# Second mixer of a two-block model: rotary queries first, rotation on GpSimd, six output rows, another order of scaling and additions

## The chip, the cores and the metric

The kernel runs on one core of a Trainium2 chip. The metric is device time in microseconds (us) of one execution. The engines are named as the profile names them: PE (TensorE matrix products, with PEld its weight loads), DVE (VectorE), ACT (ScalarE), POOL (GpSimd) and SP (SyncE, which here only issues the transfers of weights).

## The reference

Two blocks of a small model are computed for 256 tokens of width 1024, in float32. The part that the change touches is the second mixer of the second block: attention over compressed keys and values (six heads), attention over a memory (four heads), a product with an output matrix whose result is added to x, and the norm that the next feed-forward network starts with.

```python
cq, q_mem = split(rms_norm(x, mix_norm) @ b_w_in, [256])
q = (rms_norm(cq, b_q_norm) @ b_w_uq).reshape(b, s, 6, 128 + 64)
q_nope, q_rope = split(q, [128])
q_rope = apply_rope(q_rope, cos, sin)        # x1*c - x2*s, x1*s + x2*c
# six heads, in blocks of 128 queries, causal by chunks of 64
sc = (q_nope @ k_nope.T + q_rope @ k_rope.T) * 192 ** -0.5
o_b = softmax(where(mask, sc, -inf)) @ v
# four heads over 256 memory tokens
o_m = softmax(q_mem @ k_mem.T * 64 ** -0.5) @ v_mem
x = x + concat(o_b, o_m) @ w_out             # 1024 x 1024
x = x + 0.5 * swiglu(rms_norm(x, ffn2_norm), w_gu, w_down)
```

## The kernel before

**Products in three parts.** Features lie on the 128 partitions and the 256 tokens along a row. Each large product is exact float32 put together from three fast products: a value is split into a rounded high part and the rest (`_hi`, `_lo`), and `triple` (L1742) issues high times high, low times high and high times low into one bank. ACT writes the high part (`split_hi`, L471, one copy a unit of weights), DVE subtracts it to get the low part (`split_lo`, L927). Small products (scores, turned probabilities, head outputs, the rotation) are plain float32 matmuls.

**Weights.** They stream through four slabs of raw memory, two units a slab, and rings of four units `w_hi` and `w_lo`. Unit u may be written when PE has used unit u - 4 (`unit_used`). `slot(u)` splits unit u + 4 on ACT and u + 3 on DVE. SP issues a slab when DVE has split the slab four earlier (`lo_ready`).

**Banks.** Products of tiles go to four banks `main`, tile t to bank t mod 4; `bank_of(t)` waits until tile t - 4 has been read out (`evac`). Scores go to `side0` and `side3` in turn, turned probabilities to `side1`, a head's output to `side2`.

**Order.** Nothing is scheduled by a planner: each engine executes its own list, written out by hand, and the lists meet in semaphores. Around the change the lists stand in the last part of each engine's function: ACT L872 to L908, DVE L1527 to L1594, POOL L1719 to L1731, PE L2285 to L2384.

**A head.** PE issues `scores(a)`; DVE takes the row maxima (`row_maxima`, L970; for the six heads it adds the mask in the same pass, L987); ACT exponentiates (`exps`, L507) and sums; DVE multiplies by the inverse sum (`normalise`, L1000, two multiplications at L1007); PE turns the probabilities (`turn_probs`, L1803, shown as L1812); ACT copies them out (`copy_pt`, L520); PE forms the head's output (`outputs`, L1820, shown as L1838); ACT and DVE split it (`cat_hi` L868, `cat_lo` L1538). `MEM_B` to `MEM_B + 3` are the memory heads, `MLA` to `MLA + 5` the six others.

**The output matrix.** It is laid out in eight units. The first four hold a row block each (128 input features, all eight output tiles: `out_row`), for the inputs 6, 7 (memory) and 0, 1 (heads). The other four hold, for a pair of output tiles, the inputs 2 to 5 (`out_pair`). When a pair of tiles is complete DVE adds it to x (L1585), ACT scales the sum into the next network's high input (L499) and squares it (L495), DVE makes the low input (L959) and POOL adds up the squares (L1731). The network's first unit is eight `triple`s, one for each tile of x, each waiting for its low input; behind it PE sums the squares over the partitions (`norm_sum`, L1770), and goes on with the second unit.

## Time and profile before

| what | us |
|---|---|
| median of three runs | 1303.97 (1302.57 to 1303.99) |
| the profiled execution | 1301.14 |
| its span | 1299.4 |
| busy PE | 1245.8 (96% of the span) |
| busy DVE | 868.7 (67%) |
| busy ACT | 710.7 (55%) |
| busy POOL | 121.4 (9%) |

The profile shows one execution. "Span" is from the first instruction to the last; the 1.74 us beside it lie around the kernel. PE is busy nearly throughout, and the chain that ended last runs 85% through PE and 8% through DVE. The mean granted clock of TensorE is 0.987 of full speed; its two levels are 1.2 and 2.4 GHz, and in a window of time a clock of 0.5 is the lower of them.

The second mixer lies between 1028 and 1104 us of the span. The first product that depends on the changed lists starts at 1028.77 us, the last product of the output matrix starts at 1093.05 us, and the next network's second unit starts at 1103.35 us.

### The profile page before, as it was taken

The page shows a single profiled execution, that of the slowest core. Times are in us where ns is not written, and L with a number is a line of the kernel's source. Part 1 is how long each engine was busy: PE and PEld are TensorE (multiplying, and loading weights), DVE is VectorE, ACT ScalarE, POOL GpSimd, SP SyncE. Part 2 cuts the span into 40 slices and gives each one's busy share as a digit, 9 for nine tenths or more (in the row PEclk, how much of TensorE's full clock was granted, in tenths as well). Part 3 has the DMA queues.
Part 4 walks back from the last instruction along what each step waited for, and adds up shares of the span by engine and source line. Part 5 has one row for each costly group of instructions (what it writes and reads, how often), then busy time and mean ns, then how long its engine had stood idle before and what let it go on. Part 6 is the DMA issues. An engine that isn't in the chain of part 4 may idle for free.

```text
span 1299.4 us, 26184 instructions
## 1 busy us (share of the span) xinstructions
PE 1245.8 (96%) x10128; PEld 1221.3 (94%) x10128; DVE 868.7 (67%) x1419; ACT 710.7 (55%) x1046; POOL 121.4 (9%) x128
## 2 busy tenths in 40 slices
PE   7999999999999997989999999899999988999996
PEld 6899999999999997978999999899999967999996
DVE  7576699766755896247766756866665755767654
ACT  6455556756544875544756544545454545756441
POOL 7360000000000054500000000000000001000000
PEclk9999999999999999998999999999999998999998
DMA  8535455655643353003555643555563411655620
GB/s 338 171 127 195 142 191 181 214 174 183 252 168 129 130 188 130 1 1 100 192 188 174 248 166 105 187 187 173 213 223 133 142 66 66 204 184 194 246 110 32
DMA packets 48552, 209.50 MB, mean 161 GB/s; under 512 B 3398, under 2 KB 5588, under 8 KB 44004
## 3 DMA queue, kind: packets, MB, share of 16 engines
q1 hardware_dynamic: 46992, 203.89, 45.4%
q10 hardware_dynamic: 1492, 4.68, 1.0%
q8 instruction: 45, 0.74, 0.2%
q14 instruction: 23, 0.19, 0.0%
HBM read 207.47 MB, written 1.10 MB: 161 GB/s over the span
## 4 chain that ended last, share of the span: by engine, by line
PE 85%; DVE 8%; ACT 2%; POOL 2%; issue 2%; DMA 1%; ACTq 0%; DVEq 0%; POOLq 0%
PE main L1744 25%; PE main L1746 25%; PE main L1745 25%; PE main L2114 3%; DVE w_lo L925 2%; POOL dec L1683 1%; DVE cy L1298 1%; PE side L1812 1%; PE main L2163 1%; PE side L2151 1%; PE main L2304 0%; DMA spread<-delta_rows 0%; PE main L2308 0%; PE main L2306 0%; ACT w_hi L481 0%
## 5 line engine op out<-in xcount | busy, mean ns | idle before, releaser
L1744 PE MATMUL main<-xg_hi,w_hi 128*128 128x256 f32 (+1 forms) x2000 | 567.7, 284 | 5.4 <-issue 3.4
L481 ACT ACTIVATE w_hi<-raw 128x1024 fp32r<-128x1024 f32 (+3 forms) x364 | 404.4, 1114 | 306.9 <-PE main L1746 302.0
L1745 PE MATMUL main<-xg_hi,w_lo 128*128 128x256 f32 (+1 forms) x2000 | 564.6, 282 | 0.0
L1746 PE MATMUL main<-xg_lo,w_hi 128*128 128x256 f32 (+1 forms) x2000 | 564.3, 282 | 0.0
L925 DVE TENSOR_TENSOR w_lo<-raw,w_hi 128x1024 fp32r<-128x1024 f32 (+3 forms) x364 | 467.5, 1292 | 7.6 <-ACT w_hi L481 6.7
L1744 PEld LDWEIGHTS main<-xg_hi,w_hi 128*128 128x128 f32 x2000 | 378.9, 189 | 8.2 <-issue 5.5
L1746 PEld LDWEIGHTS main<-xg_lo,w_hi 128*128 128x128 f32 x2000 | 379.8, 190 | 0.0
L1745 PEld LDWEIGHTS main<-xg_hi,w_lo 128*128 128x128 f32 x2000 | 377.0, 189 | 0.5
L1746 PE MATMUL main<-h_lo,w_hi 128*128 128x256 f32 x704 | 198.3, 282 | 0.0
L1745 PE MATMUL main<-h_hi,w_lo 128*128 128x256 f32 x704 | 198.3, 282 | 0.0
L1744 PE MATMUL main<-h_hi,w_hi 128*128 128x256 f32 x704 | 198.3, 282 | 0.0
L1744 PEld LDWEIGHTS main<-h_hi,w_hi 128*128 128x128 f32 x704 | 132.6, 188 | 0.0
L1745 PEld LDWEIGHTS main<-h_hi,w_lo 128*128 128x128 f32 x704 | 132.6, 188 | 0.0
L1746 PEld LDWEIGHTS main<-h_lo,w_hi 128*128 128x128 f32 x704 | 132.6, 188 | 0.0
L1047 DVE TENSOR_TENSOR hid<-main,rstd 128x256 f32<-128x256 f32 x88 | 37.4, 424 | 101.8 <-PE main L1746 101.8
L499 ACT ACTIVATE xg_hi<-x,par 128x256 fp32r<-128x256 f32 (+2 forms) x56 | 28.5, 509 | 107.5 <-DVE x L1201 91.6
L1201 DVE SCALAR_TENSOR_TENSOR x<-main,x 128x256 f32 (+1 forms) x40 | 17.0, 425 | 93.7 <-PE main L1746 93.7
L1047 DVE TENSOR_TENSOR gate_n<-main,rstd 128x256 f32<-128x256 f32 x88 | 37.4, 425 | 35.0 <-PE main L1746 34.2
L959 DVE SCALAR_TENSOR_TENSOR xg_lo<-x,par,xg_hi 128x256 fp32r<-128x256 f32 (+2 forms) x56 | 28.6, 512 | 34.3 <-ACT xg_hi L499 34.3
L495 ACT ACTIVATE sq<-x 128x256 f32<-128x256 f32 (+2 forms) x72 | 29.3, 406 | 40.6 <-DVE x L1201 31.2
L1683 POOL TENSOR_SCALAR dec<-spread,cols 128x128 f32<-128x128 f32 x12 | 12.0, 1007 | 367.7 <-DMA spread<-delta_rows 367.7
L1234 DVE TENSOR_TENSOR hid<-hid,gate_s 128x256 f32<-128x256 f32 x86 | 36.6, 426 | 6.7 <-ACT gate_s L665 0.9
(389 smaller groups left out, 1521.6 us busy)
## 6 DMA issues: line engine op xcount, KB each, us to landing
raw<-in_w_gu_a SPq DMA_DIRECT2D x44, 1024.0 KB, 5.2
raw<-in_w_gu_b SPq DMA_DIRECT2D x44, 1024.0 KB, 5.2
raw<-in_w_down_a SPq DMA_DIRECT2D x16, 1408.0 KB, 5.9
raw<-in_w_down_b SPq DMA_DIRECT2D x16, 1408.0 KB, 5.8
raw<-in_w_in SPq DMA_DIRECT2D x20, 1024.0 KB, 5.3
raw<-in_w_in_a SPq DMA_DIRECT2D x13, 1024.0 KB, 5.2
raw<-in_w_up SPq DMA_DIRECT2D x4, 1024.0 KB, 5.2
raw<-in_w_out SPq DMA_DIRECT2D x4, 1024.0 KB, 5.1
```

The source lines that it names most:

```text
L481: act.activation(w_hi[:, u % RING, 0:n], raw[:, s % RAW, u % 2, 0:n], ACT.Copy).then_inc(hi_ready, 1)
L495: act.activation(sq[:, c % 2, 0:n], src, ACT.Square).then_inc(sq_ready, 1)
L499: act.activation(dst, src, ACT.Copy, scale=g).then_inc(xh_ready, 1)
L925: return dve.tensor_tensor(dst, src, hi.bitcast(F32), ALU.subtract)
L959: dve.scalar_tensor_tensor(dst, src, g, hi.bitcast(F32), ALU.mult, ALU.subtract)\
L1047: return dve.tensor_tensor(dst, main[t % 4][0:rows, c:c + n], scale, ALU.mult)
L1234: dve.tensor_tensor(hid[:, t % 2, :], hid[:, t % 2, :], gate_s[:, t % 2, :], ALU.mult)\
L1683: ins = gp.tensor_scalar(dec[:, h, 0, part], spread[:, h, part], g_col[:, c, h:h + 1], None, ALU.subtract)
L1744: pe.matmul(dst, a_hi, b_hi, start=first, stop=False)
L1745: pe.matmul(dst, a_lo, b_hi, start=False, stop=False)
L1746: return pe.matmul(dst, a_hi, b_lo, start=False, stop=last)
L2114: ins = pe.matmul(dst[:, c], lhs(i), rhs(i), start=True, stop=True)
```

## The change

It alters the lists of four engines and the layout of the output matrix; the number of products stays what it was.

1. **Rotary queries first.** The stream brings `w_qrope` ahead of `w_qnope`, and PE computes the rotary queries first; the plain queries come in two halves, around the tiles of the rotation (`qnope_first`, `qrot`, `qnope_last`). A head's scores now wait for just that head's query.
2. **Rotation on GpSimd.** The multiplication by cosine and the addition, each 128 x 768, go from DVE to POOL, with a new semaphore `rope_cos`. DVE keeps the three multiplications by sine, which read PSUM.
3. **Scaling ahead of the next maximum.** In DVE's list `normalise(a)` now stands ahead of `row_maxima(a + 1)`, and between the two engines' steps a unit of weights is split earlier.
4. **Six output rows.** Six units are whole rows (inputs 6, 7, 0, 1, 2, 3) and two hold the inputs 4 and 5 for four output tiles each. PE issues half a row between `scores` and `outputs` of a head, and half a row behind its turned probabilities.
5. **Additions ahead of splits.** At the end, DVE adds pair 1 before it makes the low inputs of pair 0, and so on; ACT scales four tiles before the first square. Four units of the next network's weights are split at earlier places.

```diff
-OUT_ROWS = (6, 7, 0, 1)
-OUT_BLOCKS = ((0, 2), (1, 2), (0, 3), (1, 3), (0, 4), (1, 4), (0, 5), (1, 5))
+OUT_ROWS = (6, 7, 0, 1, 2, 3)
+OUT_LAST = (4, 5)
...
-            q0, out0 = first_unit("w_qnope"), first_unit("w_out_b")
+            r0, out0 = first_unit("w_qrope"), first_unit("w_out_b")
+            slot(r0)
             exps(MEM_B)
-            slot(q0)
+            slot(r0 + 1)
             exps(MEM_B + 1)
...
+            split_hi(out0 + 8)
             cat_hi(4, MLA + 5)
             copy_pt(MLA + 5)
             cat_hi(5, MLA + 6)
-            for j in range(4):
-                act.wait_ge(evac, FIRST_TILE["out_b"] + j + 1)
-                for m in (2 * j, 2 * j + 1):
-                    scale_hi(xg_hi[:, m, 0:SEQ], x[:, m, :], gain("ffn_b2", m))
-                    square_free(SQ0["ffn_b2"] + m)
-                    square(x[:, m, :], SEQ, SQ0["ffn_b2"] + m)
-                if j == 1:
-                    split_hi(out0 + 8)
-            for j in range(1, 4):
-                split_hi(out0 + 8 + j)
+            split_hi(out0 + 9)
...
+            for m in range(KC):
+                row_hi(m)
+                if m >= 3:
+                    row_square(m - 3)
+            split_hi(out0 + 10)
+            for m in range(5, KC):
+                row_square(m)
+            split_hi(out0 + 11)
...
-            dve.wait_ge(extra_done, 6)
-            dve.tensor_tensor(q_rope[:, :, :], q_rope[:, :, :], cos[:, :].unsqueeze(1).to_broadcast([P, 3, SEQ]),
-                              ALU.mult)
-            for i in range(3):
-                taken(rot_s[:, i, :], t + i, sin[:, :]).then_inc(evac, 1)
-            dve.wait_ge(evac, t + 3)
-            dve.tensor_tensor(q_rope[:, :, :], q_rope[:, :, :], rot_s[:, :, :], ALU.add).then_inc(rope_ready, 1)
...
             row_maxima(MLA)
+            split_lo(out0 + 2)
+            normalise(MLA)
             row_maxima(MLA + 1)
-            normalise(MLA)
             cat_lo(7, 6)
             for h in range(4):
                 split_lo(out0 + 3 + h)
+                normalise(MLA + 1 + h)
                 row_maxima(MLA + 2 + h)
-                normalise(MLA + 1 + h)
                 cat_lo(h, 7 + h)
...
+            pair_add(0)
+            pair_add(1)
+            pair_lo(0)
+            pair_add(2)
+            pair_lo(1)
+            pair_add(3)
+            pair_lo(2)
+            pair_lo(3)
+            split_lo(out0 + 10)
...
+            gp.wait_ge(extra_done, 6)
+            gp.tensor_tensor(q_rope[:, :, :], q_rope[:, :, :], cos[:, :].unsqueeze(1).to_broadcast([P, 3, SEQ]),
+                             ALU.mult).then_inc(rope_cos, 1)
+            gp.wait_ge(evac, FIRST_TILE["qrot"] + 3)
+            gp.wait_ge(rope_cos, 1)
+            gp.tensor_tensor(q_rope[:, :, :], q_rope[:, :, :], rot_s[:, :, :], ALU.add).then_inc(rope_ready, 1)
...
-            for n in range(3):
-                out_row(n, 1)
+            for n in range(4):
+                scores(MLA + 2 + n)
                 out_row(n + 1, 0)
-                scores(MLA + 2 + n)
                 outputs(MLA + n)
                 turn_probs(MLA + 1 + n)
...
+                out_row(n + 1, 1)
+            out_row(5, 0)
             outputs(MLA + 4)
             turn_probs(MLA + 5)
-            out_pair(2, 2)
-            out_pair(2, 3)
+            out_row(5, 1)
             outputs(MLA + 5)
             for j in range(3):
                 out_pair(j, 4)
             for j in range(3):
                 out_pair(j, 5)
-            for k in range(2, 6):
-                out_pair(3, k)
+            out_pair(3, 4)
+            out_pair(3, 5)
```

**A head's turn on DVE.** The list of DVE before, from one head's maxima on: L987 is the masked maximum, L1005 and L1007 the scaling of the head before, L925 the low part of a head's output (`cat_lo_b`) or of a unit of weights (`w_lo`).

```order
L987 ISA s_b_160,small_66<-side0,const_61 128x128 [waits pt_ready,scores_ready]
L987 ISA small_66 128x1
L987 ISA s_b_160,small_66<-side0,const_61 128x256
L987 ISA small_66 128x1
L994 TENSOR_TENSOR small_66<-small_66 128x2 [waits dve_chain]
L1005 RECIPROCAL small_66<-small_66 128x2 [waits exp_ready]
L1007 TENSOR_SCALAR s_b_160<-s_b_160,small_66 128x128 [waits dve_chain]
L1007 TENSOR_SCALAR s_b_160<-s_b_160,small_66 128x256
L925 TENSOR_TENSOR cat_lo_b_159<-side2,cat_hi_b_165 128x256 [waits cat_hi_ready]
L925 TENSOR_TENSOR w_lo_54<-raw_52,w_hi_53 128x1024 [waits hi_ready]
```

The same stretch of the changed list, where the lines are 9 higher:

```order
L934 TENSOR_TENSOR w_lo_54<-raw_52,w_hi_53 128x1024 [waits hi_ready]
L1014 RECIPROCAL small_66<-small_66 128x2 [waits exp_ready]
L1016 TENSOR_SCALAR s_b_160<-s_b_160,small_66 128x128 [waits dve_chain]
L1016 TENSOR_SCALAR s_b_160<-s_b_160,small_66 128x256
L996 ISA s_b_160,small_66<-side0,const_61 128x128 [waits pt_ready,scores_ready]
L996 ISA small_66 128x1
L996 ISA s_b_160,small_66<-side0,const_61 128x256
L996 ISA small_66 128x1
L1003 TENSOR_TENSOR small_66<-small_66 128x2 [waits dve_chain]
L934 TENSOR_TENSOR cat_lo_b_159<-side2,cat_hi_b_165 128x256 [waits cat_hi_ready]
```

The scaling of a head stood behind the wait for the next head's scores (`scores_ready`) and now stands ahead of it.

**The rotation.** DVE before, between the last memory head's scaling and the first masked maximum (`q_rope` the rotary queries, `rot_s` their turned copy times sine):

```order
L1007 TENSOR_SCALAR s_b_160<-s_b_160,small_66 128x256
L1559 TENSOR_TENSOR q_rope_164<-q_rope_164,cos_64 128x768 [waits extra_done]
L1047 TENSOR_TENSOR rot_s_157<-main2,sin_65 128x256
L1047 TENSOR_TENSOR rot_s_157<-main3,sin_65 128x256
L1047 TENSOR_TENSOR rot_s_157<-main0,sin_65 128x256
L1564 TENSOR_TENSOR q_rope_164<-q_rope_164,rot_s_157 128x768 [waits evac]
L1566 TENSOR_SCALAR small_66<-small_66 128x2 [waits q_scaled]
```

DVE in the changed kernel, two heads earlier, behind the maximum of the third memory head:

```order
L1014 RECIPROCAL small_66<-small_66 128x2 [waits exp_ready]
L1016 TENSOR_SCALAR s_b_160<-s_b_160,small_66 128x256 [waits dve_chain]
L1016 TENSOR_SCALAR s_b_160<-s_b_160,small_66 128x256
L1056 TENSOR_TENSOR rot_s_157<-main3,sin_65 128x256 [waits extra_done]
L1056 TENSOR_TENSOR rot_s_157<-main0,sin_65 128x256 [waits extra_done]
L1056 TENSOR_TENSOR rot_s_157<-main1,sin_65 128x256 [waits extra_done]
L1568 TENSOR_SCALAR small_66<-small_66 128x2 [waits q_scaled]
L1014 RECIPROCAL small_66<-small_66 128x2 [waits exp_ready,dve_chain]
L1016 TENSOR_SCALAR s_b_160<-s_b_160,small_66 128x256 [waits dve_chain]
```

And POOL in the changed kernel:

```order
L1746 TENSOR_TENSOR small_66<-small_66 128x2 [waits q_var,cleared]
L1748 TENSOR_TENSOR q_rope_164<-q_rope_164,cos_64 128x768 [waits extra_done]
L1752 TENSOR_TENSOR q_rope_164<-q_rope_164,rot_s_157 128x768 [waits rope_cos,evac]
L1760 TENSOR_TENSOR acc_55<-acc_55,sq_56 128x256 [waits acc_done,sq_ready,acc_clear]
L1760 TENSOR_TENSOR acc_55<-acc_55,sq_56 128x256 [waits acc_done,sq_ready] x7
```

The two operations of 768 elements a row left DVE's list; on POOL the first may start when PE has turned all three tiles (`extra_done`), the second when DVE has written `rot_s`. On DVE the scaling of two memory heads (L1016) stands beside them.

**The end.** DVE before, from the last head on:

```order
L925 TENSOR_TENSOR cat_lo_b_159<-side2,cat_hi_b_165 128x256 [waits cat_hi_ready]
L946 MEMSET acc_55 128x272 [waits ss_ready]
L1585 TENSOR_TENSOR x_49<-main1,x_49 128x512 [waits unit_used,acc_clear]
L959 SCALAR_TENSOR_TENSOR xg_lo_51<-x_49,par_60,xg_hi_50 128x256 [waits xh_ready,evac]
L959 SCALAR_TENSOR_TENSOR xg_lo_51<-x_49,par_60,xg_hi_50 128x256 [waits xh_ready]
L1585 TENSOR_TENSOR x_49<-main2,x_49 128x512 [waits unit_used]
L959 SCALAR_TENSOR_TENSOR xg_lo_51<-x_49,par_60,xg_hi_50 128x256 [waits xh_ready,evac]
L959 SCALAR_TENSOR_TENSOR xg_lo_51<-x_49,par_60,xg_hi_50 128x256 [waits xh_ready]
L925 TENSOR_TENSOR w_lo_54<-raw_52,w_hi_53 128x1024 [waits hi_ready]
L1585 TENSOR_TENSOR x_49<-main3,x_49 128x512 [waits unit_used]
```

DVE in the changed kernel:

```order
L934 TENSOR_TENSOR cat_lo_b_159<-side2,cat_hi_b_165 128x256 [waits cat_hi_ready]
L955 MEMSET acc_55 128x272 [waits ss_ready]
L934 TENSOR_TENSOR w_lo_54<-raw_52,w_hi_53 128x1024 [waits hi_ready,acc_clear]
L1600 TENSOR_TENSOR x_49<-main1,x_49 128x512 [waits pair_done]
L1600 TENSOR_TENSOR x_49<-main2,x_49 128x512 [waits unit_used]
L968 SCALAR_TENSOR_TENSOR xg_lo_51<-x_49,par_60,xg_hi_50 128x256 [waits xh_ready,evac]
L968 SCALAR_TENSOR_TENSOR xg_lo_51<-x_49,par_60,xg_hi_50 128x256 [waits xh_ready]
L1600 TENSOR_TENSOR x_49<-main3,x_49 128x512 [waits pair_done]
L968 SCALAR_TENSOR_TENSOR xg_lo_51<-x_49,par_60,xg_hi_50 128x256 [waits xh_ready,evac]
L968 SCALAR_TENSOR_TENSOR xg_lo_51<-x_49,par_60,xg_hi_50 128x256 [waits xh_ready]
```

The unit of weights that stood among the additions is now split ahead of them, and the next pair's addition stands ahead of the low inputs of the pair before.

## Rows read from the trace of the kernel before

**Rows 1.** Busy time by stretch: start:end, length, engines, PE clock, DMA, GB/s.

```profile
1028.77:1093.17 64.40, 56.05 (x392) 49.88 (x391) 37.58 (x109) 29.49 (x73) 2.18 (x3) 1.00 0.30 101
1093.17:1103.35 10.18, 6.45 (x29) 5.04 (x27) 7.37 (x11) 7.20 (x15) 4.56 (x6) 0.71 0.01 2
1097.36:1104.18 6.82, 6.10 (x24) 4.81 (x23) 5.23 (x7) 5.71 (x12) 3.05 (x4) 0.51 0.01 2
```

**Rows 2.** Waits of PE, 1028.77 to 1093.2: us in total, times, longest.

```profile
PE side L1812 <- DVE s_b L1007: 6.7, 7, 1.7
```

**Rows 3.** Timeline of PE around one head, and later: start, us, instruction, idle before.

```profile
1061.99 0.55 PE L1812 MATMUL side<-const,s_b 128*128 128x128 f32 x3 [0.94 <-DVE s_b L1007]
1062.29 0.36 PE L2304 MATMUL main<-cat_hi_b,w_hi 128*128 128x256 f32 x1
...
1065.22 0.39 PE L1790 MATMUL side<-k_nope,q_nope 128*128 128x128 f32 x2
...
1066.53 0.82 PE L1838 MATMUL side<-pt_b,v_mla 128*128 128x256 f32 x4
1068.29 0.55 PE L1812 MATMUL side<-const,s_b 128*128 128x128 f32 x3 [0.94 <-DVE s_b L1007]
...
1082.99 0.81 PE L1838 MATMUL side<-pt_b,v_mla 128*128 128x256 f32 x4
1083.64 0.49 PE L1812 MATMUL side<-const,s_b 128*128 128x128 f32 x3
```

**Rows 4.** Timeline of DVE, the same head: maximum, scaling, weights.

```profile
1066.73 0.29 DVE L987 CUSTOM_DVE_ANT_0 s_b<-side,const 128x128 f32<-128x128 f32 x1 [2.40 <-PE side L1791]
...
1067.68 0.55 DVE L1007 TENSOR_SCALAR s_b<-s_b,small 128x128 f32<-128x128 f32 x2
```

**Rows 5.** Timeline of PE, two stalls in the memory heads, the rotation's tiles.

```profile
1044.44 0.66 PE L1812 MATMUL side<-const,s_b 128*128 128x128 f32 x4 [1.70 <-DVE s_b L1007]
1044.94 1.46 PE L2237 MATMUL main<-q_rope,const 128*128 128x256 f32 x6
...
1047.55 1.05 PE L1838 MATMUL side<-pt_b,mem_v 128*64 128x256 f32 x4 [1.16 <-DVE cat_lo_b L925]
```

**Rows 6.** Timeline of DVE: query copies, a memory head's maximum, the rotation's multiplication.

```profile
1035.36 1.08 DVE L1530 COPY q_nope<-main 128x256 f32<-128x256 f32 x3
...
1037.48 0.69 DVE L981 TENSOR_REDUCE small<-side 128x2 f32<-128x512 f32 x1
...
1048.05 0.95 DVE L1559 TENSOR_TENSOR q_rope<-q_rope,cos 128x768 f32<-128x768 f32 x1
```

**Rows 7.** Timeline of DVE in an earlier mixer: scalings beside and without POOL.

```profile
67.12 1.36 DVE L1007 TENSOR_SCALAR s<-s,small 128x144 f32<-128x144 f32 x2
...
76.00 0.56 DVE L1007 TENSOR_SCALAR s<-s,small 128x144 f32<-128x144 f32 x2
```

**Rows 8.** Timeline of POOL: beside that scaling, a 768-wide multiplication, two sums of squares.

```profile
67.10 1.23 POOL L1653 TENSOR_TENSOR bias<-const,cb 128x144 f32<-128x144 f32 x2 [2.57 <-DVE small L997]
...
504.74 2.27 POOL L1697 TENSOR_TENSOR kqv<-kqv,spread 128x768 f32<-128x768 f32 x1 [11.79 <-PE side L2085]
...
1100.37 1.67 POOL L1731 TENSOR_TENSOR acc<-acc,sq 128x256 f32<-128x256 f32 x2 [0.94 <-ACT sq L495]
```

**Rows 9.** Timeline of PE: the first product of the next network.

```profile
1096.33 0.36 PE L1744 MATMUL main<-xg_hi,w_hi 128*128 128x256 f32 x1 [3.00 <-issue]
```

**Rows 10.** Timeline of DVE at the end: addition to x, two low inputs.

```profile
1089.17 0.69 DVE L1585 TENSOR_TENSOR x<-main,x 128x512 f32<-128x512 f32 x1 [1.79 <-PE main L2308]
1090.51 0.49 DVE L959 SCALAR_TENSOR_TENSOR xg_lo<-x,par,xg_hi 128x256 fp32r<-128x256 f32 x1 [0.65 <-ACT xg_hi L499]
1091.14 0.73 DVE L959 SCALAR_TENSOR_TENSOR xg_lo<-x,par,xg_hi 128x256 fp32r<-128x256 f32 x1 [0.15 <-ACT xg_hi L499]
```

**Rows 11.** Timeline of ACT at the end: scaled tile, square.

```profile
1089.90 0.51 ACT L499 ACTIVATE xg_hi<-x,par 128x256 fp32r<-128x256 f32 x1 [3.26 <-DVE x L1585]
1090.31 0.40 ACT L495 ACTIVATE sq<-x 128x256 f32<-128x256 f32 x1
```

More of the change, by code:

```diff
@@ L2301, in out_block @@
             def out_block(u, b, k, m):
[L2303 removed]
+                first, last = k == OUT_ROWS[0] and m % 2 == 0, k == OUT_LAST[-1]
                 pe.matmul(out_tile[m], piece(w_hi, u, b), cat_hi_b[:, k, :], start=first, stop=False,
@@ L2334, in _ @@
+                if k == OUT_LAST[-1]:
+                    if j % 2 == 0:
+                        ins.then_inc(pair_done, 1)
+                    else:
+                        unit_end(ins)
             pe.wait_ge(lat_ready, 3)
+            rotary(0)
+            scores(MEM_B)
+            rotary(1)
+            scores(MEM_B + 1)
             queries(0)
-            scores(MEM_B)
-            scores(MEM_B + 1)
-            queries(1)
             turn_probs(MEM_B)
             scores(MEM_B + 2)
-            rotary(0)
+            for i in range(3):
+                rotate(FIRST_TILE["qrot"] + i, q_rope[:, i, :], FIRST_TILE["qrope"] + i + 1)
```

124 lines of the change are left out of this document (64 added, 60 removed).

## The prediction

> **What bounds the kernel now.** I read the page first, for the engines' shares and the clock, and then, of the second mixer alone, the busy time by stretch, the waits of PE, the timelines of PE, DVE, POOL and ACT, and the two lists of instructions. In the mixer's body, from the first rotary or plain query at 1028.77 us to the end of the output matrix at 1093.17 us, PE is busy for 56.05 of 64.40 us at full clock [rows 1]: 8.35 us are open. Seven of its stalls, 6.7 us, are PE waiting to turn probabilities that DVE has not scaled [rows 2]; two more are a low part of a head's output and the rotated queries. A typical one: the head's output starts at 1066.53 us and the turn at 1068.29, with 0.94 us idle [rows 3]. DVE begins that scaling at 1067.68 us, behind a maximum that started at 1066.73 after DVE had stood idle for 2.40 us, waiting for the next head's scores [rows 4]. So what holds PE is the order of DVE's list, not DVE's speed (37.58 us busy of 64.40 [rows 1]).
>
> Behind the body PE needs 10.18 us until the next network's second unit, 6.45 of them busy, at a mean clock of 0.71 [rows 1]. Its first wait is 3.00 us, until 1096.33 [rows 9]: DVE splits that unit's weights only between the second and the third addition. One microsecond after PE resumed, the granted clock fell to 1.2 GHz and stayed there for 6.82 us [rows 1].
>
> **The change part by part: the body.** A stall costs more than its idle time, since the pipeline also drains: an undisturbed head output takes 0.65 us to the next turn (1082.99 to 1083.64), the stalled one 1.76 (1066.53 to 1068.29), so the loss is 1.11 us where 0.94 are shown [rows 3]. With nine stalls (each idle once in the timeline of PE; three of them are [rows 3, 5]) that adds 9 x 0.17 = 1.5 to 8.35, so 9.9 us are lost in the body.
>
> *Scaling first, half a row on either side.* A head's own work on PE is 0.30 (turn) + 2.93 (a row) + 1.31 (scores) + 0.65 (output) = 5.19 us, by the starts in [rows 3], against a period of 6.30. In the new order a head's maximum, exponentials and scaling have the time from its scores to the turn in the following round, 5.2 + 3.4 us, for a chain of some 3 us. DVE has some 3 us of work in a round of 5.2 and ACT less (their mean loads, 37.58 and 29.49 of 64.40 [rows 1], times 5.2, are 3.0 and 2.4). I expect no stall in the rounds of the six heads.
>
> *What stays.* The second set of queries now waits for copies that stand behind a maximum on DVE, and the first output row for a low part; three such small waits at 0.2 to 0.25 us, 0.7 together. PE changes more often from plain float32 to the fast products: the first fast product takes 0.30 us after a turn (1061.99 to 1062.29, turn included [rows 3]), about 0.1 more than in a run of them; six more changes make 0.6. So 9.9 - 1.3 = 8.6 us could go.
>
> *The rotation on POOL.* DVE is rid of an operation of 0.95 us [rows 6] and a second of the same size, and the stalls of 1.70 and 1.16 us before it [rows 5] lose their cause. POOL needs 2.27 us for one multiplication of this size [rows 8], so 4.5 us for two. PE asks for the result only after the third memory head's turn, some 5.5 us after it has turned the tiles, so the length itself is hidden. What is not hidden: at 67.12 us DVE's pair of scalings took 1.36 us beside two additions of POOL that ran for 1.23 us [rows 7, 8], and 0.56 us with POOL idle [rows 7]. DVE's scaling waits out nearly all of POOL's operation. In the changed order DVE reaches the scaling of the second memory head within about 0.3 us of the third turned tile, which starts POOL's multiplication (both set out from the end of the first half of the plain queries: DVE with an estimated 0.7 us left of a split of weights, 1.08 for the copies, 0.69 for the maximum [rows 6] and some 0.3 of small operations, 2.8 together; PE with a turn and a memory head's scores, about 1.3 by the shapes in [rows 3], and the three tiles, 1.46 [rows 5]). If POOL comes first, or between the two scalings, that head is scaled 2.3 us late and PE, which has only one output in hand, stands for about 2.2 us; POOL's addition then meets the scaling of the third head, DVE's list slips behind it, and the first output row waits another 1.0 us: 3.2 us in all. If DVE comes first it is 0 to 0.5 us. The bounds are 0 and 4.5 us (both operations fully in the way); I take 3.2, because the rows show the block whenever the two meet.
>
> The Trainium skill (SBUF — State Buffer, section "Who interferes with whom") says the same as a rule: VectorE and GpSimd share one pair of ports under an exclusive lock, and a tensor_scalar in its two-port mode, or an operation with two SBUF inputs, waits for the whole GpSimd instruction. The trace agrees (1.36 against 0.56 us [rows 7]). By that rule alone the scalings would lose 2 x 2.27 us [rows 8], which is the upper bound above.
>
> Body: 8.6 - 3.2 = 5.4 us.
>
> **The end.** Of the eight pieces of the last pairs (0.72 us each: 6 products at 0.12, as 24 take 2.93 [rows 3]) pair 0 now ends 4 pieces before the end E of the output matrix, where it ended 6 before. Its addition starts at E - 2.6; ACT starts 0.73 us later (1089.17 to 1089.90 [rows 10, 11]) and scales four tiles at 0.41 before the first square, so squares begin at about E - 0.2. POOL takes 8 x 0.83 = 6.7 us for them (1.67 for two [rows 8]), with about 1 us of gaps for squares held up behind a split: the sum is complete at E + 7.5. The first unit's weights are split long before, so the 3.00 us wait goes; PE starts the unit at once and then waits by pieces for low inputs, which cost 0.65 us each while POOL runs (0.73 against 0.49 us [rows 10]). It ends at about E + 5.1 and PE waits 2.4 us for the sum. With the sum itself, 0.65 us, the second unit starts at E + 8.2, against E + 10.2 before, plus 0.45 there for the slow clock that still ran until 1104.18 [rows 1].
>
> The idle time is not gone: it has moved behind the first unit. So the clock will fall again. 6.82 us at half rate cost 3.4 us if PE is dense in them and nothing if they lie in the waits; before, most of it lay in waits. I take 1.9, between. End: 10.65 - (8.2 + 1.9) = 0.5 us gained; bounds -1.0 and +2.4.
>
> **Sum.** 5.4 + 0.5 = 5.9 us, from the profiled execution's 1301.14 (span 1299.4 and 1.74 around it): 1295.2 us. The median of the runs shown is 2.83 us above that execution, which the length and place of slow-clock stretches could explain; 5.9 off 1303.97 is 1298.1. I predict **1298.0 us**. For this kernel 0.2% is 2.6 us, about what can be told from no change.
>
> Edits at no cost: the stream's new order (SP requests a slab as soon as the one four earlier is split, so the slabs swapped are both there), the split of the first output unit ahead of the first exponentials (ACT waits there for a maximum of DVE's; if that cover were gone, it would cost the split's 1 us or so), the moved splits on DVE (it has 26 us free in the body).
>
> **Rivals.** *A: no collision, or the clock holds.* DVE passes ahead of POOL, and the waits at the end are short enough. For it: POOL's start depends on PE's third tile, and a scaling pair is only 0.6 us long. Against: PE is under half busy for 6 us at the end. 8.6 - 0.4 + 2.4 = 10.6 us gained, 1293.4; with one of the two, 1295 to 1296. *B: the rounds keep waiting.* A cross wait that I overlooked (a bank, a head's low part) holds PE for 1.1 us a head in four rounds: 8.6 - 4.4 - 3.2 + 0.5 = 1.5 gained, 1302.5. In effect the reordering would not do what it says. Against: DVE and ACT have 2 us free in each round. *C: slower.* POOL's lock stops PE twice in the memory heads, 4.5 us, each gap near the 3.00 us after which the clock fell [rows 9]; the gap of 1.70 did not lower it [rows 5]. Then the body runs two stretches of 6.82 us at 1.2 GHz, of which PE loses 6.8 us: 8.6 - 4.5 - 6.8 - 1.0 (end) = -3.7, so 1307.7. It decides from a gap between 1.7 and 3.0 us on; against it, the products that surround the gap are dense.
>
> **How the numbers follow.** Forecast 0.50, own range 1296 to 1300.5; A 0.28; B 0.15; C 0.07. The range 1293.0 to 1303.0 leaves out the far half of A's best and C. Faster by over 0.2% is below 1301.4: the forecast, A and a third of B, 0.83; the same is the rest of B and a little of C, 0.11; slower 0.06.
>
> **What the profile after would show.** The rounds of the six heads at 5.2 to 5.3 us with no idle before the turns; if they are 6.3, the order was not the cause. POOL's two operations of 768 near 1038 and 1042 us at 2.3 us each, with a scaling on DVE of over 2 us beside one; if the scalings stay at 0.62 a pair, A is right. The output matrix ending 5 to 6 us earlier relative to 1028.77 (9 in A). At the end no wait before the first unit, the eight sums dense on POOL, and a wait of about 2.4 us before the sum of squares; a clock of 0.5 soon after. I am wrong if the second unit starts later than E + 10 at full clock, or if the body shows a clock below 1.

## The result, and the profile after

The kernel after takes 1292.55 us (median of 4 runs, 1292.43 to 1292.94) against 1303.98 us for the kernel before beside it (4 runs, 1302.57 to 1304.02): ratio 0.9915, 95% interval 0.9898 to 0.9933. Predicted were 1298.0 us with a range from 1293.0, so the time lies just outside on the fast side, and the gain of 11.4 us is about twice the 5.9 forecast. A second comparison, below, gave 0.9940 (0.9927 to 0.9954); the difference between the two is explained there.

The profiled execution took 1292.94 us, span 1291.2. PE was busy for 1245.7 us, as before. The busy time of the mixer's body, of the end behind it, and of the slow stretch in the end, answering to [rows 1] (same columns):

```profile
1030.07:1085.35 55.28, 54.64 (x392) 49.56 (x392) 40.54 (x109) 32.27 (x75) 5.09 (x3) 1.00 0.36 122
1085.35:1094.26 8.91, 5.43 (x28) 3.98 (x27) 6.75 (x9) 7.43 (x15) 6.97 (x8) 0.76 0.23 92
1090.00:1096.85 6.85, 4.54 (x18) 3.81 (x18) 3.58 (x3) 5.21 (x8) 3.12 (x4) 0.50 0.00 0
```

The body took 55.28 us in place of 64.40, and PE stands idle in it for 0.64 us in place of 8.35. All waits of PE from 1030 to 1095 us (us in total, times, longest), against [rows 2]:

```profile
PE side L1799 <- POOL acc L1760: 2.1, 1, 2.1
PE main L1773 <- DVE xg_lo L968: 1.4, 5, 0.4
PE main L2337 <- issue: 0.6, 1, 0.6
```

The seven waits for a scaling (`s_b`) are gone; only the third row is in the body. The rounds of the heads on PE, against [rows 3]: L1870 is a head's output, L1844 the turn, L1821 the next scores.

```profile
1062.44 0.81 PE L1870 MATMUL side<-pt_b,v_mla 128*128 128x256 f32 x4
1063.09 0.49 PE L1844 MATMUL side<-const,s_b 128*128 128x128 f32 x3
1064.85 0.38 PE L1821 MATMUL side<-k_nope,q_nope 128*128 128x128 f32 x2
...
1067.59 0.81 PE L1870 MATMUL side<-pt_b,v_mla 128*128 128x256 f32 x4
1068.24 0.49 PE L1844 MATMUL side<-const,s_b 128*128 128x128 f32 x3
```

Turn to turn is 5.15 us (1063.09 to 1068.24) where it was 6.30, output to turn 0.65 where it was 1.76. DVE's timeline in such a round, against [rows 4]: the scaling now runs 1 us ahead of the maximum, and stretches of 1.58 and 0.44 us in which DVE is idle remain.

```profile
1063.71 0.42 DVE L934 TENSOR_TENSOR cat_lo_b<-side,cat_hi_b 128x256 fp32r<-128x256 f32 x1 [1.58 <-ACT cat_hi_b L870]
1064.05 1.22 DVE L934 TENSOR_TENSOR w_lo<-raw,w_hi 128x1024 fp32r<-128x1024 f32 x1
1065.18 0.16 DVE L1014 RECIPROCAL small<-small 128x2 f32<-128x2 f32 x1
1065.37 0.55 DVE L1016 TENSOR_SCALAR s_b<-s_b,small 128x128 f32<-128x128 f32 x2
1066.36 0.29 DVE L996 CUSTOM_DVE_ANT_0 s_b<-side,const 128x128 f32<-128x128 f32 x1 [0.44 <-PE side L1822]
```

In the memory heads, where the prediction expected the collision with POOL (it answers to [rows 7, 8]), DVE:

```profile
1038.85 0.62 DVE L1016 TENSOR_SCALAR s_b<-s_b,small 128x256 f32<-128x256 f32 x2
1039.38 1.08 DVE L1056 TENSOR_TENSOR rot_s<-main,sin 128x256 f32<-128x256 f32 x3
1040.38 0.80 DVE L1568 TENSOR_SCALAR small<-small 128x2 f32<-128x2 f32 x1
1041.21 0.17 DVE L1014 RECIPROCAL small<-small 128x2 f32<-128x2 f32 x1
1041.41 2.14 DVE L1016 TENSOR_SCALAR s_b<-s_b,small 128x256 f32<-128x256 f32 x2
```

and POOL, there and at the end:

```profile
1039.17 1.98 POOL L1748 TENSOR_TENSOR q_rope<-q_rope,cos 128x768 f32<-128x768 f32 x1 [6.26 <-PE main L2269]
1041.30 1.84 POOL L1752 TENSOR_TENSOR q_rope<-q_rope,rot_s 128x768 f32<-128x768 f32 x1
1085.58 7.97 POOL L1760 TENSOR_TENSOR acc<-acc,sq 128x256 f32<-128x256 f32 x8 [42.44 <-issue]
```

The scaling of the second memory head (1038.85) started 0.32 us ahead of POOL's product and was not held. The third one (1041.41) met POOL's addition and took 2.14 us in place of 0.62, but PE turned that head only at 1044.63. What reached PE is 0.64 us before the first output row; the profile names no releaser for it, but DVE finished the low part of the head's output that the row needs at 1047.12 (1046.70 plus 0.42) and PE started the row at 1047.23, and v2 below, without the lock, has no such wait. PE at the end, against [rows 9]:

```profile
1093.61 1.22 PE L1799 MATMUL side<-acc,const 128*128 128x256 f32 x2 [2.11 <-POOL acc L1760]
1094.26 0.77 PE L1773 MATMUL main<-xg_hi,w_hi 128*128 128x256 f32 x1
```

The granted clock went to 0.50 at 1090.0 us, while PE was still at the first unit; the wait for the sum began only when PE had finished it, at 1091.5.

**A span in four parts.** For every profile I cut the span at the same instructions: `lead`, to the first rotary or plain query; `body`, from there to the start of the last product of the output matrix; `end`, from there to the second `triple` of the next network's second unit; `tail`, the rest. Each is a difference of starts in the timeline of PE; lead and tail lie outside the change, but a low clock that outlasts the end falls into the tail.

| kernel | lead | body | end | tail | span |
|---|---|---|---|---|---|
| before | 1028.77 | 64.28 | 11.07 | 195.3 | 1299.4 |
| before_again | 1031.84 | 64.26 | 10.73 | 195.5 | 1302.3 |
| after | 1030.07 | 55.16 | 10.03 | 195.9 | 1291.2 |
| after_again | 1029.22 | 55.15 | 10.05 | 196.7 | 1291.1 |
| d1_scale_first | 1029.15 | 63.22 | 11.09 | 195.6 | 1299.1 |
| u1_max_first | 1030.05 | 55.17 | 10.03 | 196.0 | 1291.2 |
| u4_whole_rows | 1030.75 | 58.56 | 10.05 | 196.6 | 1296.0 |
| u2_rope_dve | 1029.55 | 55.38 | 10.04 | 197.1 | 1292.1 |
| c1_sine_ahead | 1031.61 | 56.08 | 10.06 | 197.0 | 1294.7 |
| v2_pool_waits | 1029.40 | 54.56 | 10.03 | 197.0 | 1291.0 |
| m1_rotate_late | 1030.35 | 57.40 | 10.04 | 196.5 | 1294.3 |
| u3_end_before | 1029.78 | 55.15 | 10.34 | 195.6 | 1290.9 |
| v1_sum_shared | 1030.30 | 56.13 | 6.99 | 195.7 | 1289.1 |
| v3_both | 1031.64 | 54.54 | 7.77 | 195.7 | 1289.6 |

The body repeats within 0.02 us, while the lead, the same work in every kernel, spreads over 3.1 us. So the body is read from this table, and the times are read with their intervals.

### The profile page after: what moved, and what is told of

It is laid out like the page before. It is cut to its first block, busy times and chain, and to the rows that moved or that the text cites. A ratio compares the mean times of both kernels' runs of the same rounds, so it can differ in the third digit from the quotient of the medians.

```text
span 1291.2 us, 26190 instructions
## 1 busy us (share of the span) xinstructions
PE 1245.7 (96%) x10128; PEld 1222.2 (95%) x10128; DVE 869.3 (67%) x1417; ACT 711.6 (55%) x1046; POOL 126.9 (10%) x130
## 4 chain that ended last, share of the span: by engine, by line
PE 87%; DVE 6%; POOL 2%; issue 2%; ACT 2%; DMA 1%; ACTq 0%; POOLq 0%; DVEq 0%
PE main L1773 25%; PE main L1775 25%; PE main L1774 25%; PE main L2146 3%; DVE w_lo L934 1%; PE side L1870 1%; POOL dec L1706 1%; DVE cy L1307 1%; PE side L1844 1%; PE main L2195 1%; PE side L2183 1%; PE main L2337 1%; PE main L2341 1%; PE main L2339 1%; DMA spread<-delta_rows 0%
## 5 line engine op out<-in xcount | busy, mean ns | idle before, releaser
L481 ACT ACTIVATE w_hi<-raw 128x1024 fp32r<-128x1024 f32 (+2 forms) x364 | 404.6, 1114 | 311.9 <-PE main L1775 307.3
L934 DVE TENSOR_TENSOR w_lo<-raw,w_hi 128x1024 fp32r<-128x1024 f32 (+2 forms) x364 | 467.8, 1292 | 6.8 <-ACT w_hi L481 6.0
```

The costliest lines, as they stand in the source:

```text
L481: act.activation(w_hi[:, u % RING, 0:n], raw[:, s % RAW, u % 2, 0:n], ACT.Copy).then_inc(hi_ready, 1)
L934: return dve.tensor_tensor(dst, src, hi.bitcast(F32), ALU.subtract)
```

## The experiments

Every ratio is to the kernel before, from runs beside it.

**before_again**, the kernel before, unchanged.

> The kernel before, unchanged: where its median lies 2.83 us above the profiled execution of 1301.14. Theory: the stretches of 1.2 GHz outside the mixer lie otherwise in most executions; this profile shows 1303 to 1304 and a mixer of the same 270.6 us from the first rotary query's start to the end, with the difference in front of it, by the granted clock. Rival: the mixer itself varies (its low stretch of 6.8 us at the end placed over denser work), and the part in front is the same.

Measured 1302.60 us (11 runs), ratio 1.000 (0.9991 to 1.0009). Body 64.26 us, as in the first profile; the 2.9 us between the two spans stand in the lead (3.07). By stretches of 100 us up to 1000 us, the granted clock of the two differs in two of them, 100 to 200 and 500 to 600 us; first the kernel before, then its repeat:

```profile
100.00:200.00 100.00, 97.94 (x816) 97.28 (x815) 74.03 (x114) 56.20 (x73) 0.26 (x2) 1.00 0.53 181
500.00:600.00 100.00, 89.44 (x678) 82.66 (x678) 47.25 (x93) 46.55 (x92) 32.40 (x23) 0.90 0.08 29
```

```profile
100.00:200.00 100.00, 97.97 (x801) 97.26 (x800) 72.69 (x111) 54.81 (x72) 0.45 (x2) 0.98 0.53 182
500.00:600.00 100.00, 89.93 (x670) 83.27 (x669) 47.26 (x93) 46.39 (x94) 32.40 (x23) 0.88 0.09 33
```

Fifteen products fewer fit into the first stretch (clock 0.98 against 1.00) and eight fewer into the second (0.88 against 0.90). The profiles of c1 and v3 have the same two lower clocks, and with before_again they are the only three with a lead over 1031 us. The theory holds: this is not of the mixer.

**after_again**, the kernel after, unchanged.

> The kernel after, unchanged, for a gain with a narrower interval and a second profile of the race in the memory heads. The span from the first rotary product to the last of the output matrix is 55.2 us when VectorE's second scaling starts ahead of GpSimd's product (three profiles so far) and 56.1 when it doesn't (two); the gap between the two starts is 0.3 us. Expected: 1292.5 to 1293.2, 9.5 to 10 us under the kernel before, since the runs of before in the two latest groups have medians of 1302.6 and 1302.8. Rival: 11 us or more, the first comparison's figure.

Measured 1294.89 us (5 runs, 1292.88 to 1296.30), ratio 0.9940 (0.9927 to 0.9954): a gain of 7.9 us, not the 9.5 to 10 expected, while the body is 55.15 again. The nine runs of this kernel spread from 1292.4 to 1296.3 us, with a mean granted clock of 0.987 at 1292.4 to 1292.9 (four runs) and 0.985 at 1296.3 (one). The 48 runs of before beside the four groups of these experiments go the same way: twelve at 0.987 have a median of 1301.5, twenty-one at 0.985 one of 1303.5. At 0.987 on both sides the gain is 1301.5 - 1292.6 = 8.9 us. By this estimate the 11.4 us of the first comparison hold some 2.5 us of slow stretches that fell well for the kernel after.

**d1_scale_first**: the exchange of scaling and maximum alone, in the kernel before.

```diff
             for h in range(4):
                 split_lo(out0 + 3 + h)
-                row_maxima(MLA + 2 + h)
                 normalise(MLA + 1 + h)
+                row_maxima(MLA + 2 + h)
```

> The kernel before, with one pair of lines exchanged: in the rounds of the heads VectorE scales head MLA+1+h before it takes the maximum of head MLA+2+h. Order theory (the prediction's): the head that is to be turned has had its exponentials for 2 us or more when VectorE stands idle for the next scores, so the scaling fills that idle time and the waits before the turns of the six heads vanish. Five stalls of about 1.1 us with the drain go, the round falls from 6.30 to about 5.2 us: 5 to 5.5 us off, 1298.5 to 1299 us by the median. Rival (half rows carry the gain): without half a row behind the output, the scores come too late for maximum and exponentials of the next head, a new wait of 0.5 us or more stands before the next turn and the round falls to 5.7 or so: at most 3 us off, 1301.

Measured 1301.88 us, ratio 0.9994 (0.9985 to 1.0003): nothing that the times can tell; body 63.22, 1.06 us shorter. The waits of PE in the body (us in total, times, longest):

```profile
PE side L1812 <- DVE s_b L1007: 2.9, 3, 1.7
PE main L2304 <- DVE cat_lo_b L925: 2.9, 4, 1.2
PE side L1838 <- DVE cat_lo_b L925: 1.2, 1, 1.2
```

Four waits for a scaling (6.7 to 2.9 us) have turned into four for the low part of a head's output. One of them, on PE:

```profile
1066.56 0.82 PE L1838 MATMUL side<-pt_b,v_mla 128*128 128x256 f32 x4
1067.21 0.49 PE L1812 MATMUL side<-const,s_b 128*128 128x128 f32 x3
...
1069.68 0.36 PE L2304 MATMUL main<-cat_hi_b,w_hi 128*128 128x256 f32 x1 [0.55 <-DVE cat_lo_b L925]
```

The turn comes at once, but the row that needs the head's output stands half a row behind it and waits. In the kernel before, the wait at the turn hid this one. The round falls from 6.30 to 5.95 us only. The order theory is right that the exchange takes away the waits before these turns, and wrong about what that is worth; the rival is nearer, though it named another wait.

**u1_max_first**: the same exchange undone in the kernel after.

```diff
             for h in range(4):
                 split_lo(out0 + 3 + h)
-                normalise(MLA + 1 + h)
                 row_maxima(MLA + 2 + h)
+                normalise(MLA + 1 + h)
                 cat_lo(h, 7 + h)
```

> The kernel after, with that exchange undone alone: the maximum of head MLA+2+h first, then the scaling of MLA+1+h; half rows stay on both sides of the scores. If the half rows alone cover the chain (by the rows of before: maximum 0.85 and scaling 0.75 from the scores' end, 1.75 us with the hand-over, against a half row of 1.5 and an output of 0.6 on PE) no wait returns: 1292.5, within 0.2 us. If the order of scaling and maximum is what carries it, PE waits 0.3 to 0.9 us again before each of six turns: 1294.5 to 1298.

Measured 1293.11 us, ratio 0.9933 (0.9919 to 0.9947), body 55.17: nothing lost. With half rows the exchange is worth nothing.

**u4_whole_rows**: PE's half rows put together again, in the kernel after.

```diff
-            out_row(0, 1)
             outputs(MEM_B + 3)
             turn_probs(MLA)
             for n in range(4):
+                out_row(n, 1)
+                out_row(n + 1, 0)
                 scores(MLA + 2 + n)
-                out_row(n + 1, 0)
                 outputs(MLA + n)
                 turn_probs(MLA + 1 + n)
-                out_row(n + 1, 1)
+            out_row(4, 1)
             out_row(5, 0)
```

> The kernel after, with one thing undone in TensorE's list: no half row between a head's scores and the output before it; both halves stand together ahead of the scores, as in the kernel before. Scaling stays ahead of the maximum. Theory from the exchange on the kernel before (the half rows carry the gain of the rounds): the low part of a head's output comes late, 0.56 us idle and a round of 5.95 in place of 5.15 us; four rounds, 3.2 us: 1295.5 to 1296. Rival (the earlier splits and the scaling order carry it in this kernel): 1293.

Measured 1298.07 us, ratio 0.9963 (0.9950 to 0.9977), body 58.56: 3.4 us longer. PE in its rounds:

```profile
1064.83 0.49 PE L1844 MATMUL side<-const,s_b 128*128 128x128 f32 x3
1067.30 0.36 PE L2337 MATMUL main<-cat_hi_b,w_hi 128*128 128x256 f32 x1 [0.55 <-DVE cat_lo_b L934]
...
1070.76 0.49 PE L1844 MATMUL side<-const,s_b 128*128 128x128 f32 x3
```

The round is 5.93 us, and the wait is that of d1. This kernel has the earlier splits of weights too, so they are not what shortens the rounds. The half rows carry the gain of the rounds: they stand between scores and turn, and between a head's output and the row that needs it.

**u2_rope_dve**: the rotation back on DVE, in the kernel after.

```diff
+            dve.wait_ge(extra_done, 6)
+            dve.tensor_tensor(q_rope[:, :, :], q_rope[:, :, :], cos[:, :].unsqueeze(1).to_broadcast([P, 3, SEQ]),
+                              ALU.mult)
             for i in range(3):
-                dve.wait_ge(extra_done, 4 + i)
                 taken(rot_s[:, i, :], t + i, sin[:, :]).then_inc(evac, 1)
+            dve.wait_ge(evac, t + 3)
+            dve.tensor_tensor(q_rope[:, :, :], q_rope[:, :, :], rot_s[:, :, :], ALU.add).then_inc(rope_ready, 1)
...
-            gp.wait_ge(extra_done, 6)
...
```

> The kernel after, with the two rotary operations of 768 elements back on VectorE (0.95 and 0.96 us there), none on GpSimd. Theory (VectorE passed ahead of GpSimd's lock, and only a knock-on of 0.64 us before the first output row is left): VectorE's scaling of the third memory head falls back from 2.14 to 0.62 us, but it has 1.9 us more of its own; PE's rotary queries may come 0 to 0.5 us later or earlier: 1292 to 1293.2, no change within 0.2%. Rival (moving the rotation is a large part of the gain): PE waits again 1 us or more for the rotated queries, 1294 to 1296. Rival (the lock costs more than it saves): 1291 or less.

Measured 1293.89 us, ratio 0.9931 (0.9917 to 0.9945), body 55.38: 0.2 us longer. All three scalings take 0.62 us, and PE waits 0.58 us for a bank in place of 0.64 for the row. The move to POOL gained 0.2 us, not the 1 us or more of the rival (0.8 where the lock is kept out, by the body of v2 below, 54.56).

**c1_sine_ahead**: DVE delayed by one product, so that POOL comes first, in the kernel after.

```diff
             row_maxima(MEM_B + 2)
-            normalise(MEM_B + 1)
             t = FIRST_TILE["qrot"]
             for i in range(3):
                 dve.wait_ge(extra_done, 4 + i)
                 taken(rot_s[:, i, :], t + i, sin[:, :]).then_inc(evac, 1)
+                if i == 0:
+                    normalise(MEM_B + 1)
```

> The kernel after, with the first sine product (0.45 us) moved ahead of the scaling of the second memory head on VectorE, so that GpSimd's product of 768 elements starts just before that scaling. Lock theory (the prediction's): the scaling pair, 0.62 us now, takes 2 us or more, PE stands 1.6 to 2.2 us before the turn of that head, and GpSimd's addition then meets the third head's scaling: body 1.5 to 3.2 us longer, 1294 to 1295.5. Rival (a scaling that starts beside a running GpSimd operation is not held as a whole; the 2.14 us of the other were something else): 1292.5 to 1293, the pair under 1.2 us.

Measured 1296.68 us, ratio 0.9953 (0.9939 to 0.9966), body 56.08. The scalings of the second and the third memory head on DVE, POOL's product beside the first of them, and PE's turn:

```profile
1040.72 2.17 DVE L1016 TENSOR_SCALAR s_b<-s_b,small 128x256 f32<-128x256 f32 x2
...
1043.87 2.02 DVE L1016 TENSOR_SCALAR s_b<-s_b,small 128x256 f32<-128x256 f32 x2
```

```profile
1040.67 1.81 POOL L1749 TENSOR_TENSOR q_rope<-q_rope,cos 128x768 f32<-128x768 f32 x1 [6.22 <-PE main L2270]
```

```profile
1042.95 0.66 PE L1845 MATMUL side<-const,s_b 128*128 128x128 f32 x4 [1.35 <-DVE s_b L1016]
```

The mechanism of the prediction is there: the first pair was held for 2.17 - 0.62 = 1.55 us. But PE loses 1.35 us at the turn and nothing behind it: the body is 0.93 us longer than after's, not 1.5 to 3.2. The rest of the 1296.7 us lies in lead and tail.

**v2_pool_waits**: POOL waits for the two scalings, in the kernel after.

```diff
             gp.wait_ge(extra_done, 6)
+            gp.wait_ge(probs_ready, 2 * (MEM_B + 1) + 2)
...
             gp.wait_ge(rope_cos, 1)
+            gp.wait_ge(probs_ready, 2 * (MEM_B + 2) + 2)
```

> The kernel after, with two waits added on GpSimd: its product waits for VectorE's scaling of the second memory head, its addition for the scaling of the third. Both scalings then run without the lock. If the lock is what is left in the memory heads: pairs of 0.62 us, no 0.64 us wait before the first output row, body 54.4 to 54.6 us against 55.2 (race won) and 56.1 (lost): 1291.7 to 1292.2. Rival (GpSimd's late result holds TensorE before the first head's scores): 1293 or more.

Measured 1293.32 us, ratio 0.9926 (0.9913 to 0.9940), beside after_again at 0.9940. Body 54.56 with no wait of PE left in it: the lock cost 0.59 us in the kernel after, and 56.08 - 54.56 = 1.5 us where POOL comes first. The time came out 1.1 us above the range, with a tail of 197.0; as the intervals overlap, the times don't show the 0.59 us, only the body does.

**m1_rotate_late**: the rotation's products behind the next turn, in PE's list of the kernel after.

```diff
-            for i in range(3):
-                rotate(FIRST_TILE["qrot"] + i, q_rope[:, i, :], FIRST_TILE["qrope"] + i + 1)
             outputs(MEM_B)
             turn_probs(MEM_B + 1)
+            for i in range(3):
+                rotate(FIRST_TILE["qrot"] + i, q_rope[:, i, :], FIRST_TILE["qrope"] + i + 1)
```

> The kernel after, with the six products of the rotation moved in TensorE's list from ahead of the first memory head's output to behind the second head's turn; nothing else. It asks what they are worth as cover between a head's scores and its turn, and it makes GpSimd's product start behind VectorE's second scaling for certain. Theory (what lies between scores and turn is what the memory heads gain too): in the trace of after the scores of the third head end at 1037.6 us, the output takes 1.0 us and the scaling of the second head ends at 1039.5, so TensorE waits 0.9 us before the turn; GpSimd starts 2.4 us later, its addition ends about 1045.4, close to where the first head's scores want it (1045.3, 0.9 later now), which may cost a further 0 to 0.8 us. Body 56.0 to 56.9 us against 55.15, kernel 1294 to 1296. Rival (the lock is what costs in the memory heads, and it is avoided now): no wait before the turn longer than 0.3 us, scaling pairs of 0.62, body 54.6 to 55.2 and the kernel 1292.5 or less.

Measured 1295.29 us, ratio 0.9941 (0.9927 to 0.9954), body 57.40, 2.25 us longer. The waits of PE that lie in the body, from the list of 1026 to 1100 us:

```profile
PE main L2337 <- DVE w_lo L934: 1.6, 1, 1.6
...
PE side L1844 <- DVE s_b L1016: 0.8, 1, 0.8
PE main L1773 <- DVE rot_s L1056: 0.3, 1, 0.3
```

The wait before the turn is the one expected (0.76 us). The larger one was not: the first row waited 1.56 us for a split that DVE started 2.24 us later, counted from the first query, than in the kernel after. Of that, 1.27 us is the later start of the sine products, which waited for PE's tiles, 0.21 their longer run, and 0.77 the operation on two elements behind them, which took 1.57 us beside POOL in place of 0.80. The third scaling met POOL's addition, but as it did in the kernel after (2.12 and 2.14 us).

**u3_end_before**: the order at the end undone, in the kernel after.

```diff
-            pair_add(0)
-            pair_add(1)
-            pair_lo(0)
-            pair_add(2)
-            pair_lo(1)
-            pair_add(3)
-            pair_lo(2)
-            pair_lo(3)
+            for j in range(4):
+                pair_add(j)
+                pair_lo(j)
...
             for m in range(KC):
                 row_hi(m)
-                if m >= 3:
-                    row_square(m - 3)
+                row_square(m)
             split_hi(out0 + 10)
-            for m in range(5, KC):
-                row_square(m)
```

> The kernel after, with the order at the end of the output matrix undone alone (VectorE adds and splits pair by pair; ScalarE takes high part and square in turn, the two weight splits behind them). By the prediction the new order at the end gains 0.5 us net (between -1.0 and +2.4): the wait of 3.0 us before the first unit returns, the one before the sum of squares goes: 1293.0, within 1292.3 and 1294.5. Rival (the additions ahead of the splits carry a large part of the 11.4): 1295 or more. Rival (the move only shifts the wait): same within 0.3 us.

Measured 1293.24 us, ratio 0.9930 (0.9916 to 0.9943). End and tail together take 205.97 us, against 205.97 and 206.73 in the two profiles of after. The wait before the first unit does not come back, since the weights stay split ahead of the additions; in its place PE waits 3.1 us in four pieces within the unit, and none for the sum. The order only shifts the wait.

**v1_sum_shared**: squares earlier, two of the eight additions on DVE.

```diff
                 row_hi(m)
-                if m >= 3:
-                    row_square(m - 3)
+                if m >= 1:
+                    row_square(m - 1)
+            row_square(KC - 1)
             split_hi(out0 + 10)
-            for m in range(5, KC):
-                row_square(m)
...
             pair_lo(3)
+            for m in (KC - 2, KC - 1):
+                add(SEQ, SQ0["ffn_b2"] + m)
             split_lo(out0 + 10)
...
-            for m in range(KC):
+            for m in range(KC - 2):
```

> The kernel after, with the squares drawn forward (the first after the second scaled tile, all ahead of the two weight splits on ScalarE) and the last two of the eight additions of squares on VectorE in place of GpSimd. If the wait of 2.1 us before the sum of squares is set by GpSimd's eight additions of 0.83 us and their late start, it falls below 1 us and the kernel gains 1 to 2 us: 1290.5 to 1291.5. Rival (VectorE is the one that is late there: its splits of low parts and the lock beside GpSimd move the wait into the first unit): 1292.5 to 1293.5, with waits in the unit of 0.5 us or more each.

Measured 1290.24 us (1288.32 to 1292.00), ratio 0.9902 (0.9887 to 0.9917). POOL's six additions, DVE's two, and the sum on PE:

```profile
1085.97 5.36 POOL L1761 TENSOR_TENSOR acc<-acc,sq 128x256 f32<-128x256 f32 x6 [41.74 <-issue]
```

```profile
1091.54 0.94 DVE L962 TENSOR_TENSOR acc<-acc,sq 128x256 f32<-128x256 f32 x2
```

```profile
1092.54 0.70 PE L1800 MATMUL side<-acc,const 128*128 128x256 f32 x2 [0.25 <-DVE acc L962]
```

The wait of 2.11 us is 0.25, the clock stays at full speed, and the end is 6.99 us in place of 10.03. In this profile the race in the memory heads went the other way (body 56.13):

```profile
1039.08 2.24 DVE L1015 TENSOR_SCALAR s_b<-s_b,small 128x256 f32<-128x256 f32 x2
```

```profile
1039.36 1.81 POOL L1749 TENSOR_TENSOR q_rope<-q_rope,cos 128x768 f32<-128x768 f32 x1 [6.22 <-PE main L2270]
```

POOL started 0.28 us behind the first of the two scalings and so ahead of the second, which it held (0.35 us for the first, 1.97 for the second).

**v3_both**: the waits of v2 and the end of v1 together; no other edit.

> Those two waits together with the end in which the squares are drawn forward and two of the eight additions are VectorE's. The two places are 40 us apart, so the gains should add: body 54.5 us where that kernel's profile showed 56.1 (its race was lost), end 7.0 us as there with the clock held: 1288 to 1289. Rival (without the stall in the body the clock falls elsewhere, or the end's phases shift so that a wait returns): 1290.

Measured 1291.17 us (1290.16 to 1291.35), ratio 0.9906 (0.9891 to 0.9921): the time missed the 1288 to 1289 expected and lies nearer the rival. Body 54.54 as expected, end 7.77 in place of 7.0: here the clock fell at the end of the first unit, for some 3 us (windows of 2 us at the same place, v3_both, then v1_sum_shared):

```profile
1092.00:1094.00 2.00, 2.00 (x8) 1.60 (x8) 1.46 (x2) 1.98 (x3) 0.00 (x0) 0.50 0.00 0
1094.00:1096.00 2.00, 2.00 (x15) 2.00 (x15) 0.75 (x1) 1.97 (x3) 0.00 (x0) 0.76 0.00 0
```

```profile
1092.00:1094.00 2.00, 1.75 (x13) 1.50 (x12) 1.65 (x2) 1.98 (x3) 0.00 (x0) 1.00 0.00 0
1094.00:1096.00 2.00, 2.00 (x19) 2.00 (x18) 0.50 (x1) 1.97 (x3) 0.00 (x0) 1.00 0.00 0
```

Both versions beat the kernel before, and their intervals lie below that of after_again, but overlap with the first comparison's (0.9898 to 0.9933). From the first query to the end v3 has the shortest time of all (258.0 us; v1 258.8; after 261.1 and 261.9), but the times don't tell v1 and v3 apart.

## Why the prediction was right or wrong

**The sign and the places were right.** The stalls of the body vanished, the wait at the end moved behind the first unit, and the clock fell near there again. The reason given for the clock, idle time that had moved behind the first unit, is not borne out: in after the clock fell 1.5 us before that wait began, with no gap of PE above 0.38 us at the end before it, and in v3 it fell with no wait for the sum. So the gap of 1.7 to 3.0 us from which rival C lets the clock fall was not needed here. Rival A came true by half, DVE ahead but the clock lower; its figure for that, 1295 to 1296, was above the measured time too.

**The step that failed is the term for the lock on VectorE.** The prediction took 3.2 us, "If POOL comes first, or between the two scalings". Two things were off. First, the race: in both profiles of the kernel after DVE came first. POOL's product started 0.32 and 0.31 us behind the first scaling, and in v1 at 0.28 it got in between. The prediction put both arrivals within 0.3 us of each other, which can't decide this; that the kernel after fell on the cheap side was luck. Second, the price: 0.59 us with DVE first (v2 against after), just above the 0 to 0.5 of the prediction, and 1.5 to 1.6 us with POOL first or between (c1 against v2, v1 against v3), half of the 3.2. The prediction had the scaling 2.3 us late, by a row of POOL with another product (2.27 us); this one took 1.81 us alone and held the pair for 1.55 to 1.62. PE had one output in hand, as foreseen, and waited 1.35 us (c1) and 1.08 (v1), where 2.2 were charged. The 1.0 us foreseen behind the third scaling is 0.64 in after and 0 in c1 and v1. This term accounts for 2.6 us of the body's error.

The Trainium skill (SBUF — State Buffer, section "Who interferes with whom") says that the order of issue decides which of the two engines stands, and that the other blocks fully. These traces agree: when POOL started first or between the pair, the pair took 2.0 to 2.2 us; when DVE's second scaling was ahead, POOL's product took 1.98 in place of 1.81 us. As a bound on the engine's loss the rule was right; it says nothing about what PE loses.

**"What stays", 1.3 us, was too high.** Body loss before was estimated at 9.9 us. With the lock out of the way it fell by 64.28 - 54.56 = 9.7, so 0.2 us stayed; 1.1 us of the error. In all the body gained 9.12 us where 5.4 were forecast.

**Right number, half of the cause, in the rounds.** 5.2 to 5.3 us with no idle was forecast and 5.15 measured. "What holds PE is the order of DVE's list" is true of the wait that the profile before shows, but not of the round: d1 changes that order alone, takes that wait away and gains 0.35 us a round, u1 undoes it and loses nothing, u4 undoes the half rows and loses 0.8 us a round. The prediction named half rows and order together; the half rows are enough, the order is not. In the memory heads m1 shows the same for one place: products between scores and turn are the cover. How the rest of the memory heads' gain divides among the order of queries and the earlier splits was not isolated.

**The end was right within its bounds.** Sum complete at E + 7.5 was forecast, with E the end of the output matrix; it was E + 8.2 (1093.55 - 1085.35). The wait was forecast at 2.4 us and was 2.11 (2.5 in the second profile). The second unit started at E + 8.9, not 8.2. End and tail together: 206.35 and 206.20 before, 205.97 and 206.73 after, so about 0 in place of the 0.5 gained.

**The base.** By parts the gain is 9.1 us, and 8.9 by runs at an equal clock. The rest of the 11.4 us, over 2 us, is put down to where slow-clock stretches fell outside the mixer, argued from the mean clocks of the runs and from the leads, since only two of these runs have a trace: the four runs of after were at the fast end of its nine, and those of before had a median 1.2 us above that of the 48 later ones. The prediction saw the spread of before (2.83 us) and left it out of the range; a range of that width added below would have held the time.

## What to carry to other kernels

When two waits stand in a row on the bound engine, removing the one that the profile shows uncovers the other: ask for each product when its input would be ready if PE came on time, and put independent work into both gaps. A lock between two engines is priced by the slack that the bound engine has at that place: a scaling held for 1.5 us cost PE 1.35 us where one output was in hand, and 0.64 or nothing where PE turned the head some 3 us after the scaling would have been ready. Where the two starts lie within 0.3 us a semaphore that fixes the order is worth more than an estimate. Where identical work ahead of the change spreads over 3 us, judge a change of this size by the stretch that it touches.

## What the hardware showed that was not expected

- The outcome of the race turned on a few hundredths of a microsecond: POOL's product started 0.32 and 0.31 us behind the first scaling in the profiles of after, 0.30 in u1, 0.32 in u3, 0.31 in u4 (DVE's pair 0.62 each time), and 0.28 in v1 (2.24).
- Even a `TENSOR_SCALAR` on two elements a partition waits for POOL: 0.80 us in after and 1.09 in v2, where it took 0.16 in u2 with POOL idle. The sine products, which read one operand from PSUM, took 1.08 us for three beside POOL and without it.
- At the end, PE was busy for 1.33 and 1.47 of 2 us (1088 to 1090 and 1090 to 1092) in v1 and stayed at full clock; in v3 it was busy for 1.39 and 1.49, and its clock fell within the second of these windows (mean 0.88) to 0.50. What tips it stays open.
